# Three engines walk orders of their own through the two attention stages, and the softmax minimum is carried from chunk to chunk

## The reference, cut to what matters

```
xn = rmsnorm(x);  z = xn @ w_in                       # one projection, columns shared by A and B
A: latent attention, 8 heads of 64+32:                # prompt: causal softmax over 1024 keys
   s = q_nope.k_nope + q_rope.k_rope                  # samples: paged latent cache, 2048 + 8 keys
   p = softmax(mask(s * 96**-0.5));  o = p @ v
B: dilated windows (128,1), (512,4), (2048,16), 8 heads of 64, rotary, merged by denominators
   p = softmax(mask(s * 64**-0.5));  o = p @ v        # samples: a window cache of 2048 rows
h = x + concat(A, B) @ w_out
y = h + (silu(conv3(rmsnorm(h) @ w_gate)) * (rmsnorm(h) @ w_up)) @ w_down
```

## Time and profile before

| | |
|---|---|
| median of 3 runs | 1998.89 us (1998.84 to 1999.7) |
| the profiled execution: its own time | 1998.15 us |
| the profiled execution: its span | 1996.6 us |
| PE busy over the span | 1777.9 us (89%) |
| DVE, ACT, POOL busy | 896.7, 652.3, 571.5 us |
| stage A, by its first and last work | about 277 to 617 us |
| stage B | about 617 to 1035 us |

### The profile page before, as it was taken

How to read it: one execution, slowest core, us unless ns; L and a number is a source line. 1 busy time by engine, 2 the same in 40 slices (tenths; PEclk the granted TensorE clock), 3 DMA queues, 4 the chain that set the end, 5 groups by cost and what they waited for, 6 DMA issues and landing times. The chain is left out here.

```text
span 1996.6 us, 27887 instructions
## 1 busy us (share of the span) xinstructions
PE 1777.9 (89%) x9955; PEld 1549.3 (78%) x9955; DVE 896.7 (45%) x1858; ACT 652.3 (33%) x1321; POOL 571.5 (29%) x533
## 2 busy tenths in 40 slices
PE   3999968888996878886969969999999999999997
PEld 2888857777875766776757859889889888888885
DVE  5333325566664666565743412332332333333335
ACT  4222115556554544544432212112211211211212
POOL 0000003554552446564630012212212311321211
PEclk9999988899987988998979979999999999999999
DMA  7222133233106553543334127488578659668632
GB/s 237 102 101 92 70 98 87 57 89 89 45 6 160 145 155 94 162 114 110 92 128 153 27 78 144 117 156 127 129 138 135 137 121 161 123 126 177 107 74 94
DMA packets 156106, 227.41 MB, mean 114 GB/s; under 512 B 31111, under 2 KB 129032, under 8 KB 149576
## 3 DMA queue, kind: packets, MB, share of 16 engines
q1 hardware_dynamic: 153134, 159.39, 26.8%
q0 software_dynamic: 2880, 66.85, 20.7%
HBM read 201.12 MB, written 91.93 MB: 147 GB/s over the span
## 5 line engine op out<-in xcount | busy, mean ns | idle before, releaser
L2168 DVE TENSOR_TENSOR acc<-f_dp,acc 128x512 f32<-128x512 f32 x198 | 136.5, 691 | 197.9 <-PE f_dp L2249 197.9
L2039 POOL TENSOR_TENSOR f_gl<-f_graw,f_gh 128x1024 fp32r<-128x1024 f32 x22 | 52.9, 2404 | 378.8 <-ACT f_gh L2083 378.8
L2249 PE MATMUL f_dp<-f_dh,f_ah 128*128 128x512 f32 x396 | 155.4, 392 | 4.6 <-DVE f_al L2199 4.0
L2249 PE MATMUL f_dp<-f_dl,f_ah 128*128 128x512 f32 x396 | 154.9, 391 | 0.0
L2249 PE MATMUL f_dp<-f_dh,f_al 128*128 128x512 f32 x396 | 154.7, 391 | 0.0
L2182 DVE SCALAR_TENSOR_TENSOR f_gc<-f_gp,f_coef,f_gc 128x832 f32<-128x832 f32 x44 | 47.7, 1085 | 233.4 <-ACT f_lasts L2103 230.5
L523 PE MATMUL zp<-win_h,xT_h 128*128 128x512 f32 (+1 forms) x288 | 112.7, 391 | 0.0
L1550 POOL TENSOR_TENSOR w_vl<-w_v,w_vh 96x2048 fp32r<-96x2048 f32 (+3 forms) x32 | 111.2, 3486 | 2.0
L523 PE MATMUL zp<-win_l,xT_h 128*128 128x512 f32 (+1 forms) x288 | 111.4, 387 | 0.0
L523 PE MATMUL zp<-win_h,xT_l 128*128 128x512 f32 (+1 forms) x288 | 111.3, 386 | 0.0
L768 POOL TENSOR_SCALAR l_pr<-l_pr,l_rden 128x128 f32<-128x128 f32 (+7 forms) x64 | 47.0, 746 | 172.1 <-DVE l_rden L868 172.1
(11 more groups left out here) (343 smaller groups left out, 4886.6 us busy)
## 6 DMA issues: line engine op xcount, KB each, us to landing
out_s_win_k<-in_state_win_k POOLq DMA_DIRECT2D x10, 3264.0 KB, 43.5
out_s_win_v<-in_state_win_v POOLq DMA_DIRECT2D x10, 3264.0 KB, 46.0
w_k<-in_state_win_k SPq DMA_DIRECT2D x16, 768.0 KB, 7.2
w_v<-in_state_win_v SPq DMA_DIRECT2D x16, 768.0 KB, 5.6
f_graw<-in_w_gate SPq DMA_DIRECT2D x22, 512.0 KB, 4.4
f_uraw<-in_w_up SPq DMA_DIRECT2D x22, 512.0 KB, 4.9
f_draw<-in_w_down SPq DMA_DIRECT2D x11, 1024.0 KB, 34.5
m_c<-in_cache_kv_latent SPq DMA_DIRECT2D x128, 64.0 KB, 1.8
```

The lines of the kernel that those rows point to most:

```text
L2039: nc.gpsimd.tensor_tensor(w_lo[n][:], w_raw[n][:], w_hi[n][:].bitcast(F32), ALU.subtract)\
L2168: nc.vector.tensor_tensor(a, dp[h][:], a, ALU.add).then_inc(S["d_add"], 1)
L2249: last = nc.tensor.matmul(dp[h][:], a[:, c, t * P:(t + 1) * P], w[:, c, h * 512:(h + 1) * 512], start=(c == 0 and j == 0), stop=(c == 1 an ...
```

## The change

There are four parts.

1. Every engine gets a list of its own. `turns_of` starts from the common list and adds to the place of an event a number that depends on the engine, the side and the kind of event; SyncE and TensorE have none. `Ring.plan` counts each engine's semaphore steps along its own list. A few waits are added on ScalarE that say in the code what the common order had implied.
2. The minimum is carried on. A chunk's VectorE instruction starts from the minimum of the chunk before instead of from 3e38, so that the last chunk leaves the row's minimum. L864, L1233 and L1626 are gone, and `exp` waits for the last chunk of its own head.
3. The copy of `l_kh` into `l_kl` is an event `swap` of its own, done by ScalarE.
4. In A the common list itself changes: `rT` of a group stands behind `cT`, `s`, `exp` and `rows` rather than ahead of `cT`.

```diff
-            if what == 1:
-                self.ring.done(dve, e)
-                nc.vector.tensor_copy(lo[0:HD, :, cols], hi[HD:P, :, cols]).then_inc(S["k_ok"], 1)
+        elif e[0] == "swap":
+            _, n, f = e
+            cols = slice(f * 512, f * 512 + 512)
+            self.ring.done(act, ("prep", n, 1, 0, f))
+            nc.scalar.copy(self.kl[0:HD, :, cols], self.kh[HD:P, :, cols]).then_inc(S["k_ok"], 1)
...
-                if last:
-                    act.wait_ge(S["min"], k // PT * 4 + s - 3)
-                else:
-                    self.ring.done(act, ("score", k, h, 0))
+                self.ring.done(act, ("score", k, h, last))
...
+            low = HUGE
+            if c:
+                self.ring.done(dve, ("score", k, h, 0))
+                low = self.nm[:, k % 2, 0, h:h + 1]
             dve.sem_inc(S["neg_go"])
             nc.vector.tensor_tensor_reduce(
-                out=self.pr[:, k % 2, h, c0:c0 + w], in0=bank[:, 0:w], in1=tab, scale=-self.scale, scalar=HUGE,
+                out=self.pr[:, k % 2, h, c0:c0 + w], in0=bank[:, 0:w], in1=tab, scale=-self.scale, scalar=low,
                 op0=ALU.add, op1=ALU.min, accum_out=self.nm[:, k % 2, c, h:h + 1]).then_inc(R["bank_d"], 1)
-        elif e[0] == "exp":
...
-                m = self.nm[:, k % 2]
-                nc.vector.tensor_tensor(m[:, 2, :], m[:, 0, :], m[:, 1, :], ALU.min).then_inc(S["min"], 1)
...
             if b < B:
-                E.append((("rT", g), 0.45))
                 E.append((("cT", g), 0.45))
...
-            if b < B and g + 1 < 4 * B:
-                E.append((("rows", g + 1), 0))
+            if b < B:
+                if g + 1 < 4 * B:
+                    E.append((("rows", g + 1), 0))
+                E.append((("rT", g), 0.45))
...
+def turns_of(order, later):
+
+    return {eng: [x for _, x in sorted(((n + later.get(eng, {}).get((x[0], x[1][0]), 0), x) for n, x in enumerate(order)),
+                                       key=lambda at: at[0])]
+            for eng in ("sync", "gpsimd", "scalar", "vector", "tensor")}
+
+LATENT_LATER = {
+    "gpsimd": {(0, "over"): 13, (1, "rows"): -11},
...
+DILATED_LATER = {
+    "gpsimd": {(0, "over"): 7, (1, "v_split"): -9},
+    "scalar": {(0, "out"): 3, (0, "swap"): 4, (1, "exp"): 2, (1, "k_turn"): -1, (1, "q_block"): 19},
+    "vector": {(0, "out"): -2, (0, "over"): -2, (0, "score"): -1, (1, "k_turn"): 1, (1, "score"): 1,
+        (1, "value"): 2},
+}
...
-            for i, e in order:
+            for i, e in turns["gpsimd"]:
                 sides[i].gpsimd(pool, e)
```

More of the change, by code:

```diff
@@ L573, in __init__, with plan @@
         self.use, self.by, self.free, self.high = {}, [], {}, {}
-    def plan(self, order, sides):
-        count = {"bank_d": 0, "bank_a": 0, "bank_hi": 0}
-        for i, e in order:
[L578 to L588, removed]
+    def plan(self, turns, sides):
+        used = {eng: [(e, sides[i].bank_use(e)) for i, e in turns[eng] if sides[i].bank_use(e)]
+                for eng in ("tensor", "scalar", "vector")}
+        self.by = [e for e, _ in used["tensor"]]
+        self.use = {e: u for u, e in enumerate(self.by)}
+        self.high = {e: n + 1 for n, e in enumerate(e for e, kind in used["scalar"] if kind == "hd")}
+        self.free = {e: ("bank_a", n + 1) for n, e in enumerate(e for e, kind in used["scalar"] if kind == "a")}
+        self.free |= {e: ("bank_d", n + 1) for n, e in enumerate(e for e, kind in used["vector"] if kind != "a")}
     def take(self, pe, e):
@@ L641, in __init__ @@
         self.S = {n: sem(t(n)) for n in (
-            "table q_in0 q_in1 k_in0 k_in1 v_in k_lo k_ok v_hi v_lo neg_go min exp recip norm o_ps o_a o_d o_out0 o_out1 sink").split()}
+            "table q_in0 q_in1 k_in0 k_in1 v_in k_lo k_ok v_hi v_lo neg_go exp recip norm o_ps o_a o_d o_out0 o_out1 sink").split()}
         self.units = [(s + 2) // 2 for s in range(PT)]
@@ L660, in prep @@
                 E.append((("prep", n, what, h, f), 0.45))
+            if self.kind == 1 and what == 1:
+                E.append((("swap", n, f), 0))
         def score(k, c, h):
@@ L785, in scalar @@
             hi, bank = (self.qh, self.kh)[what], self.ring.ready(act, e)
+            if n:
+                last = n * PT - 1
+                self.ring.ready(act, ("score", last - 4, 1, 0) if what == 0 and f == 0 else ("score", last, 1, f))
             if self.kind == 0:
@@ L1398, in _ @@
         def _(sp):
-            for i, e in order:
+            for i, e in turns["sync"]:
                 sides[i].sync(sp, e)
@@ L1410, in _ @@
         def _(act):
-            for i, e in order:
+            for i, e in turns["scalar"]:
                 sides[i].scalar(act, e)
@@ L1415, in _ @@
         def _(dve):
-            for i, e in order:
+            for i, e in turns["vector"]:
                 sides[i].vector(dve, e)
@@ L1420, in _ @@
         def _(pe):
-            for i, e in order:
+            for i, e in turns["tensor"]:
                 sides[i].tensor(pe, e)
@@ L1617, in vector @@
                 self.ring.ready(dve, ("p_turn", b - 2, 1))
+            low = HUGE
+            if u:
+                dve.wait_ge(S["s_free"], 3 * b + u)
+                low = self.st[rows, u - 1:u]
             dve.sem_inc(S["neg_go"])
@@ L1620, in vector @@
                 out=self.pr[rows, cols], in0=self.SC[rows, 0:w], in1=self.window[rows, cols], scale=-DIL_SCALE,
[L1621 to L1626 removed]
+                scalar=low, op0=ALU.add, op1=ALU.min, accum_out=self.st[rows, u:u + 1]).then_inc(S["s_free"], 1)
         elif e[0] == "p_turn":
```

62 lines of the change are left out of this document (30 added, 32 removed).

## The result

The kernel after takes 1893.8 us (median of 4 runs, 1891.86 to 1896.09), the kernel before 1998.87 us beside it (4 runs, 1998.83 to 1999.7): a ratio of 0.9474, 95% interval 0.9457 to 0.949.

A forecast was written before the change was run, and what follows sets the result against it. TensorE sets the time, with slack only in stages A and B (138.1 us idle). Savings of 28.5 us in A and 44 in B make 72.5; a quarter off leaves 54, so 1998.15 - 54 = 1944 us, range 1905 to 1985.

The forecast's parts named there:

- The quarter taken off: Whole sum: a quarter of 72.5 us taken off, since an earlier TensorE meets the next late operand earlier; 54 us left.
- The minimum in B: Stage B: without L864, and with the samples' first `exp` earlier, TensorE's waits fall by 12.6 us.
- The minimum in A: Stage A: the carried minimum was priced at nothing in the sum.
- The rotary keys: Stage A: GpSimd splits the rotary keys earlier, saving 14 of 16.9 us; `rT` and the earlier `exp` save 2 together.
- The copy: Stage B: the copy L837, moved to ScalarE at 1.14 us each, saves 12.4 us of waits.
- The order in B: Stage B: GpSimd's earlier `v_split` saves 6 us; VectorE's order and added ScalarE waits cost 1 us each.
- The clock: Stages A and B: long waits lower TensorE's clock; nine fewer at 2.5 us each save 7 and 15 us.
- nothing comes back: Rival: the sum stands whole and the order takes up some 30 us more idle time; about 1896 us, chance 0.14.
- VectorE blocks itself: Rival: VectorE stops at early `out`, `over` or blocked scores, 1.5 us lost per step; about 2022 us, chance 0.04.
- The round trips stay: Rival: waits for keys and probabilities (22.2 and 13.7 us) stay, set by ScalarE and VectorE; about 1973 us, chance 0.19.
- the `m_r` waits: Sign of a right forecast, rotary keys in stage A: no wait of TensorE for `m_r` over 1 us.
- waits on `a_pr`: Sign of a wrong forecast: new waits of TensorE on GpSimd's `a_pr`, which had none.

The follow-up runs named there:

- a1: The kernel before with only the carried minimum, for prompt and samples (no L864, L1233, L1626): 1955.64 us, ratio 0.9787.
- b3: The kernel after with the prompt's minima kept apart and joined by a VectorE instruction of two SBUF inputs: 1927.59 us, ratio 0.9662 to the kernel before.
- a2: The kernel before with only the copy into `l_kl` moved to ScalarE: 1988.3 us, ratio 0.9951.
- d4: d1 with the copy into `l_kl` back on VectorE: 1905.72 us, ratio 0.9533 to the kernel before.
- d1: The kernel after with stage A's table cut to the offsets of the samples' start, B's table whole: 1893.11 us, ratio 0.9466 to the kernel before.
- a3: The kernel after with the tables of both stages empty, the move of `rT` kept: 1918.79 us, ratio 0.9601 to the kernel before.
- b4: The kernel after with the prompt's minima kept apart and joined by a VectorE reduction of one SBUF input: 1905.06 us, ratio 0.9556 to the kernel before.
- a4: The kernel after with the copy back on VectorE and L864 back for the prompt, samples' minima still carried: 1947.08 us, ratio 0.9742 to the kernel before.
- c1: The kernel before with only `rT` moved in stage A's common list: 1980.83 us, ratio 0.9932.
- d2: d1 with stage B's table cut to GpSimd's two entries: 1902.94 us, ratio 0.9513 to the kernel before.

## Why the prediction was wrong

The direction and most of the places were right; the size was half. Each part's gain can be split as the table in the section on the result does, into TensorE's idle time and its busy time for the same matmuls, the clock (one profiled execution each, so 3 us are no finding):

| stage B | idle, forecast | idle, measured | clock, measured |
|---|---|---|---|
| minimum, alone (a1) | 12.6 | 16.6 | 15.0 |
| minimum of the prompt, taken back (b3) | | 16.4 | 14.6 |
| copy, alone (a2) | 12.4 | 9.0 | 0 |
| copy, taken back (d4 to d1) | | 10.7 | 3.2 |
| tables (a3 to d1) | 4 | 18.7 | 9.8 |
| whole change | 29 | 43.5 | 24.8 |

By the prediction's own steps:

- **The quarter taken off**, 18.5 us, is the largest item in the closing sum below. I argued that a TensorE that comes earlier meets the next late operand earlier. New waits did appear (3.4 us for `w_ktl` at L906, 5.2 for `a_pr`, 3.1 for `m_c`), but nothing is lost in the sum: TensorE's idle time in A fell by what the places had promised (20.3 for 21.5), and in B by more. Nor do the parts eat each other's gains in B: minimum 31.6 (alone) or 31.0 (taken back, b3, the prompt's only), copy 9.0 or 13.9, table 28.5, against 68.2 for all. (The 85 us of idle time that I named beside it should have been 88.)
- **The minimum in B.** I summed 12.6 us from the places where a run of L864 or the samples' first `exp` ends the chain visibly. The idle time that it ended was 16.6, not far off. With the clock in the proportion of my own sum (15 us for the 31 of these three terms) I had 19 us; measured are 31, and most of the difference is the clock, 15.0 us, as much as I had given the whole stage. The wait table had put much of this under `w_ktl`, whose subtraction stands behind the blocked L864 in VectorE's list. I had read these 22.2 us as a round trip of its own, and named this as the thing that spoke against the closest rival. The minimum alone took 12.1 of them away (a1), and b3 against b4 shows 10.2 that hang on the blocking. The mechanism was right, the term mis-sized.
- **The minimum in A** stood in the sum at nothing. Alone it is worth 11.8 us there. The prompt's part of it is worth nothing that can be measured once the table is in place (a4 310.1, b3 308.4, b4 306.6, after 309.3), and these three kernels keep the samples' minima carried. Without the table the minimum with the copy is worth 21.1 (c1 323.0, a3 301.9), and there the waits stand behind the samples' exponential and its minimum. That the samples' part gives the gain in A is likely from these rows, but no kernel took it away alone; nor does any show whether the table ends the same waits.
- **The rotary keys** came out at about the right size, but not by GpSimd's table. I gave 14 us to that table and 2 to `rT` with `exp`. The move of `rT` alone ends the waits for `m_r` (c1), and GpSimd's delayed `over` brings new ones, which I had costed at nothing. Whether the table alone would have ended them too, no kernel tested.
- **The copy**: 12.4 us and its clock, 18 by the same proportion; measured 9 to 14. Too high. Its duration was right (1.14 forecast, 1.05 measured).
- **The order in B** is the step that failed most: I took 6 us for GpSimd and charged 2 for the rest, 4 us of idle time; measured are 18.7, and 28.5 with the clock. GpSimd's entries are worth 17.7 us, and ScalarE's and VectorE's, on which I had put a loss, 11.4. These 14.7 us are as much as the whole gain in idle time of B was forecast too small (14.5); the minimum's 4 too few and the copy's 2 to 3 too many nearly cancel. Which of ScalarE's and VectorE's entries does it, no kernel separates; the waits that they end are those for the copy's result and the low probabilities (d2).
- **The clock**: 36 us for 22. I had counted nine waits, those of three microseconds and more, at 2.5 us each. Going through TensorE's waits of over 0.5 us and taking those with a mean clock under 0.9 from one to three microseconds behind them, I find 28 before and 15 after (without the two at the cuts ahead of A and behind B): 13 fewer, 2.8 us each. Ten of the 13 are of three microseconds and more (15 before, 5 after), so my count of these was nearly right, and at my price they explain 25 us; the rest is in the shorter ones and in the price. Some waits of 2 us have a drop behind them. The kernel before at 391.35 us, behind a wait of 2.08 us, and at 663.60, behind 1.98:

```profile
391.35:393.35 2.00, 2.00 (x12) 1.66 (x12) 1.26 (x7) 1.32 (x4) 1.92 (x2) 0.50 0.22 50
...
663.60:665.60 2.00, 2.00 (x7) 1.62 (x8) 1.00 (x3) 0.00 (x0) 0.84 (x1) 0.54 0.09 34
```

The sum closes: 18.5 (the quarter) + 14.0 (clock) + 14.5 (idle time in B) - 1.2 (idle time in A) + 2.3 (outside the stages) + 2.3 (the profiled execution against the median) = 50.4 us, and 1944.2 - 50.4 = 1893.8.

Of the rivals, "nothing comes back" (1896, at a chance of 0.14) is nearest to what happened: on balance nothing came back, and the order took up more of the idle time than its places had shown. Its time was right partly by luck. It had 80.5 us less idle time and 22 of clock; measured are 63.8 and 36. "VectorE blocks itself" didn't happen: a loss of 1.1 us and more at each of 64 steps would have shown as idle time, and this fell by 63.8 us. "The round trips stay" didn't either: the waits for keys and probabilities are at 13.2 us where they were 35.9 (16.6 with the 3.4 at L906). Of the signs named, the `m_r` waits, the first scores (285.99 us for about 287), the idle time in A (29.8 for 30), the clock (0.92 and 0.93) and the swap came true. The idle time in B (47.5 for 60) was lower. One sign of a wrong forecast appeared, waits on `a_pr`, and the scores with a carried minimum are not as long as the others but 52 to 64 ns longer.

Three things stay open: why the same idle time costs so much more clock for the minimum (15.0 us for 16.6) than for the copy (none for 9.0); what the samples' minima are worth by themselves; and what in A's table costs the clock there.

## What to carry to other kernels

Add up the reductions that the timeline shows and let them stand; take off something only for a named wait that will take their place. Ahead of an instruction moved back, look for one that waits for a load. Where one instruction of an engine is blocked for microseconds, count the waits on everything queued behind it as its own, also where the table of waits names another line, and try replacing a tiny instruction of two SBUF inputs by one of one input before rebuilding anything (b4 against b3: 22.5 us). When a wait has both a late producer and an early consumer, try moving the consumer: here one line in the common list ended the waits that a table for another engine was credited with. Split every measured gain into idle time and busy time before saying which step was mis-sized.

## What the runs showed of the hardware

- A VectorE minimum over 128x2 pairs of numbers took 148 to 2649 ns with two SBUF inputs and 144 to 158 ns with one, at the same place of B beside the same GpSimd work. In stage A, whose GpSimd instructions are shorter (0.67 us on average against 1.58 in B), the same two-input instruction took 151 to 809 ns.
- A starting value read from SBUF made the fused score instruction 52 to 64 ns longer, at 128 columns (344 for 292 ns on average) as at 512 (745 for 683). None of its 32 runs in B took over 751 ns beside GpSimd's work, with its one PSUM input, one SBUF table and the column.
- TensorE's clock fell to its lower level behind waits of 1.98 and 2.08 us, but not behind every wait of that length. Behind one of 3.04 us that ended at 812.05 us in the kernel before the granted clock of the next two microseconds was 1.00, and behind the one of 2.29 us that ended at 423.07 it stayed at its full level too:

```profile
423.20:425.20 2.00, 2.00 (x15) 1.86 (x15) 0.21 (x1) 2.00 (x4) 1.92 (x2) 1.00 0.20 50
```

What tells the two kinds apart, these runs don't show.
